# Value, key and query tiles in high and low halves, with low halves completed by adding DMA transfers

## The reference

```python
xn = rmsnorm(h, norm_mix_g)
proj = xn @ w_in                      # 2048 x 3584: gate pairs, q, k, v
a = proj[..., :2048]                  # gated (GLU), then a 31-tap depthwise convolution
q = partial_rope(...); k = partial_rope(...); v = ...
conv_out = silu(layernorm(depthwise_conv(a[:1024] * sigmoid(a[1024:]))))
h = h + concat(conv_out, window_attention(q, k, v)) @ w_out
mn = rmsnorm(mem, norm_mem_g); mk = mn @ w_ck; mv = mn @ w_cv    # 256 memory tokens
h = h + cross_attention(...)          # memory keys and values
h = h + peer_experts(rmsnorm(h))      # product-key retrieval over 16384 experts
```

## Time and profile before

| | us |
|---|---|
| median of 3 runs | 1991.41 (1989.99 to 1993.25) |
| profiled execution, its own time | 1991.95 |
| its span | 1990.1 |
| gate tiles 1 to 15 | 34 to 128.37 |
| value, key and query tiles | 128.37 to 221.5 |
| first attention scores at | 236.98 |

### The profile page before, as it was taken

How to read it: one execution, slowest core, us unless ns; L and a number is a source line. 1 busy time by engine, 2 the same in 40 slices (tenths; PEclk the granted TensorE clock), 3 DMA queues, 4 the chain that set the end, 5 groups by cost and what they waited for, 6 DMA issues and landing times.

```text
span 1990.1 us, 29316 instructions
## 1 busy us (share of the span) xinstructions
PE 1953.2 (98%) x11128; PEld 1753.2 (88%) x11128; DVE 1530.8 (77%) x2295; ACT 857.2 (43%) x869; POOL 723.3 (36%) x498
## 2 busy tenths in 40 slices
PE   6999999999999999999999999999999999999998
PEld 6997788998999999999999999988888888888886
DVE  4988766556788898899888997567777767777776
ACT  4340144444535555545455546434443333344343
POOL 2010101220436778888877874011110101214300
PEclk9999999999999999999999999999999999999999
DMA  5463395543444778778888998899888999999984
GB/s 210 161 203 131 100 378 214 170 169 121 155 140 157 255 280 288 284 272 295 279 282 277 312 352 293 289 337 353 335 331 324 347 340 347 366 347 354 371 312 144
DMA packets 101243, 531.29 MB, mean 267 GB/s; under 512 B 19392, under 2 KB 21600, under 8 KB 45808
## 3 DMA queue, kind: packets, MB, share of 16 engines
q1 hardware_dynamic: 71552, 408.93, 57.2%
q0 software_dynamic: 24320, 106.45, 14.8%
q10 hardware_dynamic: 5296, 14.98, 1.9%
HBM read 491.44 MB, written 38.14 MB: 266 GB/s over the span
## 4 chain that ended last, share of the span: by engine, by line
PE 92%; DVE 4%; ACT 2%; issue 1%; DMA 1%; POOL 0%; DVEq 0%; SPq 0%; ACTq 0%; POOLq 0%
PE acc L1630 20%; PE mis L2010 17%; PE acc L2010 17%; PE acc L1631 10%; PE acc L1607 5%; PE acc L1609 5%; PE acc L1608 5%; PE acc L1656 5%; PE acc L1752 2%; DVE wl L946 1%; DMA raw<-in_u 1%; PE mis L1727 1%; ACT wh L549 1%; PE mis L1703 0%; DVE xhl L954 0%
## 5 line engine op out<-in xcount | busy, mean ns | idle before, releaser
L946 DVE TENSOR_TENSOR wl<-raw,wh 128x2048 fp32r<-128x2048 f32 x310 | 711.4, 2296 | 279.1 <-ACT wh L549 277.9
L549 ACT ACTIVATE wh<-raw 128x2048 fp32r<-128x2048 f32 x310 | 593.2, 1915 | 565.8 <-DMA raw<-in_v 411.4
L1630 PE MATMUL acc<-xhl,wh 128*128 128x448 f32 x2048 | 643.2, 374 | 0.9 <-DVE wl L946 0.9
L1631 PE MATMUL acc<-xhl,wl 128*128 128x224 f32 x2048 | 541.3, 264 | 0.0
L1630 PEld LDWEIGHTS acc<-xhl,wh 128*128 128x128 f32 x2048 | 384.1, 188 | 31.2 <-DVE wl L946 1.8
L1631 PEld LDWEIGHTS acc<-xhl,wl 128*128 128x128 f32 x2048 | 390.8, 191 | 0.0
L2172 POOL DMA_INDIRECT G<-gsum,cell x224 | 362.0, 1616 | 79.1 <-issue 66.9
L1607 PE MATMUL acc<-xhl,wh 128*128 128x288 f32 x736 | 220.6, 300 | 15.1 <-DVE wl L982 14.1
L1608 PE MATMUL acc<-xhl,wh 128*128 128x288 f32 x736 | 217.7, 296 | 0.0
L1609 PE MATMUL acc<-xhl,wl 128*128 128x288 f32 x736 | 217.3, 295 | 0.0
L2128 POOL DMA_INDIRECT ring<-in_ur,eidx x32 | 45.8, 1430 | 326.3 <-DVE hs L1435 317.5
(11 more groups left out here) (339 smaller groups left out, 2632.4 us busy)
## 6 DMA issues: line engine op xcount, KB each, us to landing
raw<-in_u SPq DMA_DIRECT2D x128, 1024.0 KB
raw<-in_v SPq DMA_DIRECT2D x128, 1024.0 KB
raw<-in_w_mix SPq DMA_DIRECT2D x28, 1024.0 KB
G<-zero SPq DMA_DIRECT2D x16, 1024.0 KB, 13.7
raw<-in_w_out SPq DMA_DIRECT2D x16, 1024.0 KB
raw<-in_w_pq SPq DMA_DIRECT2D x16, 1024.0 KB
gin<-G SPq DMA_DIRECT2D x32, 512.0 KB, 8.9
h<-hbg ACTq DMA_DIRECT2D x32, 448.0 KB, 5.8
```

The lines of the kernel that those rows point to most:

```text
L549: act.activation(wh[:, n % 4], raw[:, n % 4], ACT.Copy).then_inc(hi_done, 1)
L946: dve.tensor_tensor(wl[:, n % 4], raw[:, n % 4], wh[:, n % 4].bitcast(F32), ALU.subtract).then_inc(lo_done, 1)
L1630: pe.matmul(acc[:, s, 0:2 * NU], wh[:, s, j, :], xu[:, j, 0:2 * NU], start=(j == 0), stop=False)
L1631: ins = pe.matmul(acc[:, s, 0:NU], wl[:, s, j, :], xuh[:, j, :], start=False, stop=(j == DT - 1))
```

## The change

From gate tile 4 to query tile 27 (`SUM0` to `SUM1`), the low half is no longer subtracted by VectorE. ScalarE writes two copies of each tile, `wh = raw` rounded and `wl = -raw`, rounded the same way; GpSimd then issues a DMA that adds the fp32 weights from HBM a second time into `wl`, which leaves `raw - wh` there. TensorE first issues all 32 matmuls of a tile that need `wh`, waits for that DMA (`sum_in`), and then the 16 with `wl`. The value, key and query tiles are multiplied in the same halves as all others, and `xg` goes.

VectorE's convolution is dealt out anew: 12 steps a gate tile from tile 2 on, and the other 88 over the 12 value, key and query tiles. Five rotations (`turn`, `rope`) stand between those tiles, over three banks. The sum of squares of the memory tokens is made from a second, row-wise copy of them (`mem_rows`, 2 MB more to load) by ScalarE with an accumulator, a diagonal matrix by VectorE and two small matmuls; the memory norm is taken between tiles too. The value transposes stay behind the last tile. `memT` shares memory with `wh` 2 and 3, is loaded only after tile 23, and tiles from 24 on alternate between `wh` 0 and 1. SyncE, not GpSimd, writes the convolution history out, ahead of the loads of `mem_rows` and of tile 20. The waits ahead of the attention loop for `vtok` and for the cached keys go to its step 1 and to its sample units. The halves of product-key tile 1 are made after the last part instead of after part 11, and ScalarE's half of product-key tile 4 a step earlier.

```diff
+            def both_halves(n):
+                act.wait_ge(raw_in[n % 4], 16 * (n // 4 + 1))
+                act.activation(wh[:, high_slot(n)], raw[:, n % 4], ACT.Copy).then_inc(hi_done, 1)
+                act.activation(wl[:, n % 4], raw[:, n % 4], ACT.Copy, scale=-1.0).then_inc(neg_done, 1)
...
+            for n in range(VKQ0 + 2, SUM1):
+                if n >= VKQ0 + 10:
+                    act.wait_ge(slot_used, n - 1)
+                both_halves(n)
+                if n == VKQ0 + 3:
+                    for t in range(2):
+                        act.wait_ge(memr_in[t], 16)
+                        act.activation(memr[:, t], memr[:, t], ACT.Square, accum_out=gsp[:, t:t + 1]).then_inc(mem_sq, 1)
+                if n == VKQ0 + 9:
+                    memory_gain(0)
+                    memory_gain(1)
+                if n == VKQ0 + 10:
+                    norm_root(1, mis[:, 3], mem_stat, 1, MEM)
+                    memory_gain(2)
+                    memory_gain(3)
...
+            def add_raw(n):
+                pool.wait_ge(neg_done, n - SUM0 + 1)
+                pool.dma_start(wl[:, n % 4], dr["w_mix"][n], accum_op=ALU.add).then_inc(sum_in[n % 4], 16)
+            for n in range(8):
+                if 2 * n + 2 >= SUM0:
+                    add_raw(2 * n + 2)
+                pool.wait_ge(sig_done, n + 1)
+                pool.wait_ge(acc_free, GLU0 + 4 + 2 * n)
+                if n == 0:
+                    pool.wait_ge(rstd_done, 1)
+                pool.tensor_tensor(gsb[:, 2, :], gsb[:, 1, :], rstd[:, 1, :], ALU.mult).then_inc(sgr_done, 1)
+                if 2 * n + 3 >= SUM0:
+                    add_raw(2 * n + 3)
...
+            def sum_slot(n):
+                s, h = n % 4, high_slot(n)
+                pe.wait_ge(hi_done, n + 1)
+                pe.wait_ge(acc_free, n + 1)
                 for j in range(DT):
-                    ins = pe.matmul(acc[:, n % 4, 0:N], raw[:, n % 4, j, :], xg[:, j, :], start=(j == 0), stop=(j == DT - 1))
+                    pe.matmul(acc[:, s, 0:N], wh[:, h, j, :], xh[:, j, :], start=(j == 0), stop=False)
+                    pe.matmul(acc[:, s, 0:N], wh[:, h, j, :], xl[:, j, :], start=False, stop=False)
+                pe.wait_ge(sum_in[s], 16 * (n // 4))
+                for j in range(DT):
+                    ins = pe.matmul(acc[:, s, 0:N], wl[:, s, j, :], xh[:, j, :], start=False, stop=(j == DT - 1))
                 ins.then_inc(slot_used, 1)
...
             stream("w_mix", GLU0, 1, 5)
             sp.wait_ge(slot_used, VKQ0)
+            sp.wait_ge(acc_free, VKQ0 + 4)
+            sp.wait_ge(hist_zero, 1)
+            sp.wait_ge(hist_in, 16)
+            sp.dma_start(dr["nconv_p"], glu[:, :, NP_:NP_ + HIST]).then_inc(nconv_out, 16)
+            sp.dma_start(dr["nconv_s"], glu[:, :, XW - HIST:XW]).then_inc(nconv_out, 16)
+            for n in range(2):
+                sp.dma_start(memr[:, n], dr["mem_rows"][:, n]).then_inc(memr_in[n], 16)
+            stream("w_mix", GLU0, 5, 7)
+            sp.wait_ge(slot_used, VKQ0 + 8)
             for n in range(4):
                 sp.dma_start(memT[:, 4 * n:4 * n + 4, :], dr["memT"][:, 4 * n:4 * n + 4, :]).then_inc(mem_in[n], 16)
-            stream("w_mix", GLU0, 5, 7)
...
+VKQ_TURN = {4: 0, 6: 1, 7: 2, 8: 3, 9: 4}
+VKQ_ROPE = {5: 0, 7: 1, 8: 2, 9: 3, 10: 4}
+GLU_CONV = (0, 0) + 14 * (12,)
+VKQ_CONV = (10, 10, 10, 10, 10, 7, 9, 6, 6, 6, 0, 4)
+MEM_DIAG, MEM_STAT, MEM_RECIP = 6, 8, 10
-CO_NEXT = {8: 2, 11: 3}
+CO_NEXT = {8: 2}
```

More of the change, by code:

```diff
@@ L589, in _, with memory_gain @@
             glu_iteration(0, True)
-            with act.Fori(1, 3) as i:
+            for i in (1, 2, 3):
                 glu_iteration(i)
[L592 to L596, removed]
+            def memory_gain(n):
                 act.wait_ge(mem_in[n], 16)
-                act.activation(memsq[:, at, :], memT[:, at, :], ACT.Square).then_inc(mem_sq, 1)
-                act.wait_ge(mem_sq, n + 1)
                 for m in range(4 * n, 4 * n + 4):
@@ L618, in _ @@
             padded_keys(0)
+            for n, (bank, at, ln, tiles) in enumerate(((1, 0, BAND, (3, 4)), (2, 0, P, (0, 1)), (2, 256, NS, (4, 5)), (3, 0, BAND, (1, 3)))):
+                act.wait_ge(vt_done, 3 if n == 1 else 1 + n)
+                nt = tiles[1] - tiles[0]
+                act.activation(vtok[0:ln, tiles[0]:tiles[1], :],
+                               mis[0:ln, bank, at:at + 256 * nt].rearrange("p (t c) -> p t c", t=nt), ACT.Copy).then_inc(vt_out, 1)
+            act.sem_inc(hi_done, OUT0 - SUM1)
             def attention(A, hooks):
@@ L763, in pq @@
                         norm_root(3, mis[:, 2], stat_done, 2)
-                    elif not (first and s == 1):
+                    elif not first or s == 3:
                         hi_next(PQ0, i, s)
+                    elif s == 1:
+                        hi_next(PQ0, 0, 2)
                     if i == 3 and s == 3:
@@ L1001, in conv, with conv_steps, glu_iteration @@
                         dve.wait_ge(conv_dve, ct)
[L1002 to L1005 removed]
+                    if n < 2:
+                        own.done(dve.tensor_scalar(cacc[:, n, :], x, w, None, ALU.mult))
                     else:
                         own.done(dve.scalar_tensor_tensor(cacc[:, a, :], x, w, cacc[:, a, :], ALU.mult, ALU.add))
[L1009 removed]
+            def conv_steps(done, dealt, n):
+                for m in range(done + sum(dealt[:n]), done + sum(dealt[:n + 1])):
+                    if m == 0:
+                        dve.wait_ge(hist_zero, 1)
+                        dve.wait_ge(hist_in, 16)
+                    if m % 32 == 0:
+                        dve.wait_ge(acc_free, GLU0 + 4 + 2 * (m // 32) + 2)
+                    conv(m // 32, m < 32, m % 32, m % 32 + 1)
+            def glu_iteration(i, first=False):
                 for s in range(4):
[L1011 removed]
+                    if first and s < SUM0 - AHEAD:
                         lo_next(GLU0, i, s)
@@ L1060, in q_parts @@
                 yield [one(qsm[:, ds(t, 1), :])] + [o[:, NP_:N] for o in others]
-            for n in range(12):
-                vkq(n)
             def rope(n):
                 j = ROPE[n]
-                bank = mis[:, n % 2, :] if n < ROPE_EARLY else acc[:, 0, :]
+                bank = mis[:, n % TURN_BANKS, :] if n < ROPE_EARLY else acc[:, 0, :]
                 ops = [bank[:, 0:N], sin, cos, sqt[:]]
@@ L1080, in rope @@
                 ins.then_inc(rope_done, 1)
-            for n in range(ROPE_EARLY):
-                rope(n)
+            for n in range(12):
+                vkq(n)
             def attention(A, hooks):
```

165 lines of the change are left out of this document (76 added, 89 removed).

## The result

The changed kernel takes 2012.51 us (median of 4 runs, 2009.59 to 2013.44), the kernel before 1992.33 in the same session: a ratio of 1.0099, 95% interval 1.0082 to 1.0117. It is 20 us slower. The profiled execution has a span of 2007.8 us, 17.7 more than before. The first views are the windows by stage, cut where the changed kernel's stages end, and three lines of the page: busy time, chain by engine, chain by line.

What follows compares the result with a forecast made beforehand. TensorE, busy 98% of the span, was taken as the bound. Tiles -17.6, tail -14.1, turns and norm +3.3, clock -1.5, value-stage waits +11 and product-key order -1 gave -19.9: 1971 us, range 1958 to 2010.

Steps and rivals of the forecast that it cites:

- The rival of the double price: Adding transfers: second operand's read costs as much as the first, 5 us or more each; +19, 2010 us; chance 0.27.
- the price of an adding transfer: DMA engines, each tile's low half: 3.0 us of engine time and 7.5 us from issue to landing.
- The upper bound: Adding transfer's price at twice a plain load, 5 to 6 us, since it must also read what it adds to.
- Gate stage: Adding transfers in the gate tiles: 5.9 us of DMA a tile just fits TensorE's 6.29, so 0.
- Waits of the value stage: TensorE waits at tile 20 for 6 us, tile 26 some 3, tile 27 2 more: together +11 us.
- The 12 tiles: Value, key and query tiles in halves instead of fp32: 75.5 us instead of 93.1, -17.6 us.
- The tail: Behind the last query tile only the transposes remain, about 1.4 us instead of 15.5: -14.1 us.
- The clock: First memory tiles: without the pause TensorE doesn't run slow after it, -1.5 us, between 0 and -2.
- VectorE and ScalarE: Gate stage: VectorE falls behind under 2 us over seven pairs, ScalarE stays idle 40% despite second copies: 0.
- ScalarE's in-order list: Rival: waits for `mem_rows` and `memT` ahead of later copies cost 25 us, not 11; about 1986; chance 0.17 shared.
- The product-key order: Output loop: product-key tile moved out of the middle, -1 us, between -2 and +1.

Runs made afterwards that it cites:

- run 2: Changed kernel with the adding transfers taking their addend from wh in SBUF instead of the weights in HBM (low halves cancel): 2010.33 us.
- Run 1: Changed kernel with plain transfers to a spare buffer instead of adding ones (low halves zero), memory rows loaded early: 1971.35 us.
- run 3: Changed kernel with the memory rows loaded before the gate stage and squared by ScalarE in tile 0: 2003.72 us, ratio 1.0068 to the kernel before.
- run 9: Changed kernel with memory rows early and ScalarE's scaling of the memory tokens moved behind tile 27's halves: 1999.57 us, ratio 1.0041 to the kernel before.
- run 11: Kernel before the change with only the new product-key order: 1990.63 us against 1992.13, ratio 0.9988.
- Run 4: Changed kernel without adding transfers: gate tiles by subtraction, 12 later tiles in fp32, rotations and memory norm between tiles: 1985.22 us, ratio 0.9969 to the kernel before.
- Run 12: Run 4's version with its last 16 convolution steps moved into attention steps 1 to 4: 1978.89 us, ratio 0.9941 to the kernel before.
- run 6: Changed kernel with memory rows early and the history's write-out behind the loads of tiles 20 to 23: 2004.16 us, ratio 1.0056 to the kernel before.
- run 7: Changed kernel with VectorE's subtraction back in gate tiles 4 to 15, adding transfers only in the 12 value, key and query tiles: 2006.48 us.
- run 8: Changed kernel with adding transfers on odd tiles 5 to 27 only, subtraction or fp32 on even ones, memory rows early, history written by GpSimd: 1991.75 us, ratio 0.9999.
- run 10: Run 4's version with adding transfers on odd gate tiles 5 to 15, memory rows early, history written by GpSimd: 1986.11 us, ratio 0.9965 to the kernel before.

## Why the prediction was wrong

The forecast was 1971 us, with a range of 1958 to 2010; measured were 2012.5. The rival of the double price, at 2010, had been given 0.27.

- **The step that failed** is the price of an adding transfer, "I take 3.0 us of the engines, 7.5 to landing". It measured 5.1 and 12.4. The upper bound, 5 to 6 us, was the truth; its reason, that the transfer must also read what it adds to, fits run 2 but was not separated from the addition itself. I chose between the ends by a plain load's time to landing, a row that says nothing on a second operand, and gave the upper end no weight in the sum. Run 1 shows that this one term carries the sign: with plain transfers, and the rows early, the same kernel takes 1971.35 us. The early rows, worth 9 us in run 3, are less than the 20 gained.
- **Gate stage, 0 predicted**: 14.5 us more. The rate argument was right in form, 5.9 us of DMA a tile against 6.29; with 5.1, and a load at its least, 2.5, it is 7.6, and the tiles took 7.5. The rival's +14 came within 1 us.
- **Waits of the value stage, +11 predicted**: the stage took 113.5 us, 38 more than 12 x 6.29, 3 of which are the turns. The rival had +36. The places were named rightly in part: tile 20 with 12.0 us over its work (6 predicted, 13 by the rival), tile 26 with 9.4 (3, and 10); tile 27 had only 0.8 (2, and 5). Not named were tile 17 (4.9), next to the write-out, and tile 24 (6.0): it waits for its load, while the additions that came free together behind tile 20 fill the engines for 5.1 us each.
- **The 12 tiles, -17.6**: TensorE's work did shrink. In run 1, where nothing waits, tiles 16 to 19 take 6.0 to 6.4 us each. The gain went into waiting.
- **The tail, -14.1**: 0.8 us instead of 1.4 stands there, -14.7: right. **The clock, -1.5**: the first memory tile takes 3.62 us instead of 4.85, -1.2: right. But the waits in the value stage now cost clock themselves, which no term of the sum held: the grant was 0.91 over 142.89 to 256.40 us, 0.73 in 190 to 195, after 5 us in which TensorE was busy for 0.85, which fits the 12 us by which its busy time there exceeds the work.
- **VectorE and ScalarE, 0**: right. In run 1 the gate tiles come every 6.4 us, which is the 12.8 us a pair that I had for VectorE, and TensorE is full beside it. **ScalarE's in-order list** was a rival of its own; moving the wait for `memT` in run 9 gave about 4 us.
- **The product-key order, -1**: -1.5 us in run 11, between -0.6 and -4.4.
- The two gains together, -14 for the tail and -1 for the order, should have stayed without the adding transfers. Run 4 gave 6.5 us and not 9 to 13, because five rotations between tiles move VectorE's work to where its convolution and, in that run, the gate tiles' subtractions already fill it. Run 12 let the steps lie over the attention, and 12 us came.

Left open: how long the history's write-out occupies the engines by itself. It was never run alone; run 6 shows only that moving it to another place in the same queue gains nothing. Open too is which part of an adding transfer costs, the second read or the addition.

## What to carry to other kernels

Take a price for a new operation from a row that has the operation in it; here an adding transfer cost as much as two plain ones. When the two bounds lie on both sides of the point at which the sign turns, don't let a row of the cheaper kind decide between them. DMA engines that are half idle are cover for a transfer only if rate and time to landing both fit, and on full engines, as in the value stage here, a further megabyte or a slow small transfer may be paid in TensorE's time wherever it stands in the queue (run 6). Work that is taken out of one engine's way has to fit on the next: in runs 4, 7 and 8 TensorE waited 4.0 to 6.7 us behind the last tile for VectorE's convolution, and that hid part of what the edit gave. An edit that bundles several steps should be taken apart: here the parts without the adding transfers, with VectorE's steps dealt out anew, are 12 us faster than before, while the whole is 20 us slower.

## What the runs showed that was not expected

- A transfer that adds into SBUF moved 202 to 208 GB/s with all engines busy, a plain one 426. The place of the addend made no difference: 281 GB/s in the gate stage with it in HBM, 280 in run 2 with it in SBUF.
- On engines 0.85 busy it still took 10.5 us to landing, twice its own 5.1 (runs 8 and 10); a plain one on engines 0.88 busy took 6.9 (run 1).
- The convolution history, 2 x 120 KB, took 24.5 us to landing beside adding transfers (12.1 us in run 4, without them), in windows in which the engines were full at 175 and 183 GB/s.
